# Down products of second pieces of up to 64 rows: the two output halves side by side in the columns of the array

## The reference, cut to what matters

```
def swiglu(x, w_gu, w_down):
    gate, up = jnp.split(x @ w_gu, 2, axis=-1)
    return (jax.nn.silu(gate) * up) @ w_down
```

## Time and profile before

| | |
|---|---|
| median of 3 runs | 3312.72 us (3307.3 to 3314.82) |
| the profiled execution: its own time | 3313.27 us |
| its span in the profile | 3311.2 us, so 2.1 us lie around it |
| TensorE busy | 2804.2 us, 85% of the span |
| expert stage, rank 0's products to rank 63's last | about 2250 to 3220 us of the span |
| pieces whose `down` the change touches | 34 (ranks 2 to 35) of 101 |

### The profile page before, as it was taken

How to read it: one execution, slowest core, us unless ns; L and a number is a source line. 1 busy time by engine, 2 the same in 40 slices (tenths; PEclk the granted TensorE clock), 3 DMA queues, 4 the chain that set the end, 5 groups by cost and what they waited for, 6 DMA issues and landing times. The chain is left out here.

```text
span 3311.2 us, 29374 instructions
## 1 busy us (share of the span) xinstructions
PE 2804.2 (85%) x11882; PEld 1746.9 (53%) x11882; DVE 853.1 (26%) x1550; ACT 398.8 (12%) x665; POOL 462.6 (14%) x440
## 2 busy tenths in 40 slices
PE   5998874997469668999999749988999999999981
PEld 3444433444469653444444334436767666688871
DVE  4112454331444331111112341221111111111114
ACT  1001121111222100000000000001111111111110
POOL 1000100000124100000000106002222222222211
PEclk9999995998789868999999859998999999999995
DMA  5010020000000003211301125019988888899973
GB/s 196 26 51 26 1 79 26 26 26 0 0 1 1 1 0 109 56 29 29 105 3 64 58 105 100 0 51 339 282 251 245 259 252 256 259 337 361 361 235 127
DMA packets 179163, 391.63 MB, mean 118 GB/s; under 512 B 14784, under 2 KB 53312, under 8 KB 178144
## 3 DMA queue, kind: packets, MB, share of 16 engines
q1 hardware_dynamic: 153184, 302.67, 26.5%
q0 software_dynamic: 24992, 80.21, 10.6%
q10 hardware_dynamic: 864, 7.02, 0.5%
HBM read 327.48 MB, written 62.39 MB: 118 GB/s over the span
## 5 line engine op out<-in xcount | busy, mean ns | idle before, releaser
L1725 PEld LDWEIGHTS banks<-arena 128*128 128x128 f32 x4160 | 531.6, 191 | 48.0 <-issue 42.6
L1725 PE MATMUL banks<-arena 128*128 128x128 f32 (+7 forms) x4160 | 540.7, 290 | 4.5 <-DMA arena<-in_exp_w_gu 3.7
L1733 PE MATMUL banks<-arena 128*128 128x512 f32 (+6 forms) x808 | 365.4, 594 | 17.5 <-DVE arena L1846 15.9
L1137 PE MATMUL banks<-arena 128*128 128x512 f32 x768 | 339.6, 594 | 16.0 <-DMA arena<-in_w_branch 12.6
L365 PE MATMUL banks<-arena 128*128 128x512 f32 x640 | 278.2, 596 | 1.2 <-PE banks L365 0.9
L1137 PEld LDWEIGHTS banks<-arena 128*128 128x128 f32 x768 | 144.9, 189 | 203.9 <-issue 203.9
L1673 POOL DMA_INDIRECT acc_scratch<-arena x100 | 154.3, 1543 | 699.9 <-DVE arena L1846 449.3
L1733 PEld LDWEIGHTS banks<-arena 128*128 128x128 f32 (+6 forms) x808 | 121.9, 160 | 185.5 <-issue 162.9
L365 PEld LDWEIGHTS banks<-arena 128*128 128x128 f32 x640 | 121.3, 190 | 157.3 <-issue 157.3
L1143 PE MATMUL banks<-arena 128*128 128x512 f32 x384 | 172.7, 592 | 1.1 <-DMA arena<-y_ret_scratch 1.1
L358 PE MATMUL banks<-arena 128*128 128x512 f32 x384 | 167.9, 598 | 1.6 <-PEq L284 0.9
(11 more groups left out here) (333 smaller groups left out, 2589.3 us busy)
## 6 DMA issues: line engine op xcount, KB each, us to landing
arena<-in_exp_w_gu SPq DMA_DIRECT2D x65, 2048.0 KB, 12.5
arena<-in_exp_w_down SPq DMA_DIRECT2D x65, 1024.0 KB, 10.4
arena<-in_w_in SPq DMA_DIRECT2D x10, 2048.0 KB, 9.0
arena<-in_w_in SPq DMA_DIRECT2D x24, 512.0 KB, 6.1
arena<-in_w_branch SPq DMA_DIRECT2D x24, 256.0 KB, 6.2
arena<-in_x SPq DMA_DIRECT2D x4, 1024.0 KB, 15.6
h_scratch<-arena SPq DMA_DIRECT2D x1, 4096.0 KB, 13.1
arena<-in_w_out SPq DMA_DIRECT2D x2, 2048.0 KB, 12.0
```

The source lines that it names most:

```text
L1137: last = nc.tensor.matmul(PS[:, b, :], wm[u][:, k, n, :], hT[:, k, hs], start=(k == 0), stop=(k == KD - 1))
L1725: last = nc.tensor.matmul(PS[:, bank + part, f * n:(f + 1) * n], weights[:, k, part * FF + f * P:part * FF + (f + 1) * P], by_k(x, n)[:, k ...
L1733: last = nc.tensor.matmul(PS[0:n, 6 + j, :], hid[:, f, lo:lo + n], weights[:, f, j * HALF:(j + 1) * HALF], start=(f == 0), stop=(f == 1))
```

## The change

For a second piece of up to 64 rows, `down_more` takes the place of `down`. It makes the same 4 calls with the same operands, but half 1 goes to partitions 64 to 64+n-1 of bank 6 (so its stationary operand lies in columns 64 and up of the array) instead of to bank 7, and the order of the loops is turned: f outside, j inside, so the calls alternate between the two column ranges. VectorE reads half 1 from there. The 88-row pieces, the A pieces and the spills stay as they were, and no wait is added or taken away.

```
+                def down_more(weights, hid, n):
+                    for f in range(2):
+                        for j in range(2):
+                            last = nc.tensor.matmul(PS[64 * j:64 * j + n, 6, :], hid[:, f, P:P + n], weights[:, f, j * HALF:(j + 1) * HALF],
+                                                    start=(f == 0), stop=(f == 1))
+                    return last
...
-                        down(dn[r % RING], by_f(hidT[r % 2], n), P, more(r)).then_inc(x_dn, 1)
+                        if more(r) > 64:
+                            down(dn[r % RING], by_f(hidT[r % 2], n), P, more(r)).then_inc(x_dn, 1)
+                        else:
+                            down_more(dn[r % RING], by_f(hidT[r % 2], n), more(r)).then_inc(x_dn, 1)
...
-                    nc.vector.tensor_scalar(out[r % 2][0:n, HALF:2 * HALF], PS[0:n, 7, :], gate[r % 2][0:n, :], None,
+                    src = PS[0:n, 7, :] if n > 64 else PS[64:64 + n, 6, :]
+                    nc.vector.tensor_scalar(out[r % 2][0:n, HALF:2 * HALF], src, gate[r % 2][0:n, :], None,
                                             ALU.mult).then_inc(x_yv, 1)
```

## The result

The changed kernel takes 3259.7 us (median of 4 runs, 3256.5 to 3263.8), the kernel before 3313.8 on the same occasions: ratio 0.9838, 95% interval 0.9827 to 0.985. It is 54 us faster; 43.7 were predicted (3269), and the value lies inside the range. The profiled execution is the slowest of the four, 3263.8 us, with a span of 3261.8, so against its counterpart before the gain is 49.5.

What follows compares the result with a forecast made beforehand. TensorE was taken to bound the kernel. 34 pieces x 1.29 us = 43.7 us, taken from the profiled 3313.3, gave 3269.6, and 3269 by the median; the range was 3255 to 3292.

Steps and rivals of the forecast that it cites:

- TensorE sets the pace: Expert stage: TensorE busy 97 to 99.9 of 100 us, so a microsecond saved there is one of the whole.
- 8 distances of 0.429 us and 0.10 of passage per block: `down` of B before: 8 instruction starts 0.429 us apart, 3.43 us, plus 0.10 to the next products, 3.53 in all.
- 5 distances: `down` of B after: instructions start in program order, three pairs overlap across columns, saving 1.29 us per piece.
- fourth rival: `down` of B: all of half 1 runs beside half 0, saving 1.71 us per piece, 58 us, 3255; chance 0.05.
- Entry and exit neither added to nor saved: Around B's `down`: both halves share an array division, so the 0.84 us load wait and 0.10 us cost stay.
- Weight loads: B's `down`: the same 8 loads of 0.10 to 0.135 us; if late, only 0.94 us saved per piece.
- Read-outs hidden: VectorE's 0.74 us and ScalarE's 0.68 lie behind the next rank's 8.44 us of products, costing nothing.
- The adds: GpSimd's two serial adds per rank take 14.4 us, against a shortest new rank of 15.3, so they fit.
- The output buffers leave a rank's slack, so TensorE doesn't see it: Ranks 1 and 2: adds may fall behind by a microsecond a rank for two or three ranks, without delaying TensorE.

Runs made afterwards that it cites:

- quarters: The changed kernel with second pieces of up to 32 rows split into four parts of 256 output columns at partitions 0, 32, 64, 96: 3242.7 us, ratio 0.9787.

## Why the prediction was right in kind and short in size

- *TensorE sets the pace, so its microseconds count one for one.* Right, but for 4.1 us in two ranks.
- *8 distances of 0.429 us and 0.10 of passage per block.* Right; both stand in the profile after.
- *5 distances.* This is the step that failed: "I take 5, since the order within a call rules out 4 unless the instructions are issued in another order." The order within a call holds; the order between calls of different columns doesn't. The term measured 1.69 us (57.6 / 34) where 1.29 was put. That was the fourth rival, held at 0.05. I took the rows of one stream to show that instructions start in program order; with all work on the same columns they can't show anything else.
- *Entry and exit neither added to nor saved.* Right: 0.84 us before the next load, as before. The Trainium skill's rule that a change of mode drains and a change of tile doesn't ("TensorEngine Tiling (Array Packing)", "Key Properties") now has its second half shown: half 1 and half 0 stream 8 instructions in 1.83 us without a drain between them. The 0.10 us of passage are not all the price of entry and exit: after 88 rows the block takes 3.47 us (2269.50 to 2272.97 before), so 0.04 of passage stand there too.
- *Weight loads.* None came late; they go in by pairs under the streams of both column ranges. The Trainium skill's rule cited against the change ("TensorE: Matmul & The Clock Gate", "What overlaps and what doesn't") didn't hold here: loads over the same 128 rows overlapped throughout, at the start four within 0.16 us.
- *Read-outs hidden.* Right; VectorE takes 0.75 us from partitions 64 and up, 0.74 before.
- *The adds.* 14.4 against 15.3 us was worked out with the median landing of all 100 adds before, which is too long for these ranks (5.7 there), with landings that were taken to stay as they were (7.3 after), and with a block 0.4 us too long (the rank is 14.91). The first error offset the second: two adds take 14.6 by the median after. "The output buffers leave a rank's slack, so TensorE doesn't see it" looked at the wrong buffer: what TensorE sees is the gather queued behind the adds. Cost: 3.2 us in rank 37, and perhaps the 0.9 in rank 34, whose cause stays open.
- *In sum*: 57.6 of TensorE, less 4.1 for the holes and 0.7 at rank 0, is 52.8, against 52.6 measured for the stage. By the medians the whole gained 54.0. 43.7 was short by 14 on the overlap, and nothing had been taken off for the holes. The two errors partly cancel, so that the forecast is 10 us off and not 14; that is luck.

What stays open: how many instructions TensorE can pass over (three waiting ones were passed), what made the hole of rank 34, and why adds land later, 7.3 us for 5.7, in the ranks with a B piece once these are shorter. That the DMA share rose from 0.85 to 0.93 fits, but was not varied by itself.

## What to carry to other kernels

Where a product has at most 64 stationary columns, split its moving operand and send the parts to different partition ranges (0 and 64, measured here for 8 to 64 columns; or 0, 32, 64 and 96, measured for 8 to 24 columns): the streams ran side by side, with two ranges in either order of the calls. A trace in which every product uses the same columns says nothing about the order in which others may start, so a bound from that order deserves more than 0.05. When a rank gets shorter, compare its new length with every serial chain that runs once or twice per rank, by the landing time of the ranks in question and not by a median over all of them, and look at what else is issued from the queue that waits.

## What the hardware showed that I had not expected

- MATMULs with different output partition ranges start out of program order: half 1's first instruction began with half 0's first, past three that were waiting (1.84 us for 8 instructions of 512 columns, in either loop order).
- Four streams of 256 columns at once, float32, didn't hold each other up: 16 instructions in 0.99 us, against 0.86 for 4 distances of 0.215, half of the 0.43 of a stream of 512 columns. One stream of 256 columns alone was not measured.
- A chain that fills nearly the whole rank needn't show where it does so: with quarters, 20 ranks of 14 to 15 us ran without a hole on TensorE, and the holes (2.2 and 0.65 us) came in ranks 37 and 38, the second and third without a B piece.
